# The first input chunk of a decoder trunk in two token halves, its conditioning sums first, and two loads on ScalarE's DMA queue

## Chip, cores and metric

The kernel runs on one core of one Trainium2 chip. The metric is the device time of one launch in microseconds (us): the median of several runs. The program is written directly for the engines: TensorE (PE), VectorE (DVE), ScalarE (ACT), GpSimd (POOL) and SyncE (SP), each with its own stream of instructions, tied to the others by semaphores alone.

## What is computed

A causal decoder trunk of two layers on one sequence: `x` is 512 tokens by 1024, `c` one conditioning vector of 1024, everything in f32. Each layer has a mixer and a SwiGLU feed-forward part, and each of these takes an input that is scaled and shifted by numbers computed from `c`:

```python
c_act = jax.nn.silu(c)
mod = c_act @ ada_w[layer] + ada_b[layer]
sh_m, sc_m, g_m, sh_f, sc_f, g_f = [t[:, None, :] for t in jnp.split(mod, 6, axis=-1)]
hm = x * (1.0 + sc_m) + sh_m
y = gla_mlstm_mixer(hm, ...)        # layer 0; it begins with proj = h @ w_in
x = layer_norm(RES_ALPHA * x + (1.0 + g_m) * y, ...)
```

The mixer of layer 0 (gated linear attention beside an mLSTM) and of layer 1 (stick-breaking beside dilated attention), the feed-forward parts and the norms behind them are not touched. What matters here is the very start: before the first projection can run, `silu(c)` has to be multiplied with the shift and scale blocks of `ada_w[0]` (1024 x 1024 each), and `x` has to be scaled.

## The kernel before

**Layout and arithmetic.** The hidden input h is kept transposed: 1024 features are eight chunks (KC = 8) of 128 partitions, each with 512 tokens. Every f32 product is made of three faster ones: h and the weights are split in a high part in the type fp32r and a low part that is the rest. So for each chunk ACT makes `tmp` (scaled x, L815) and `h_hi` (a copy in fp32r, L800), and DVE makes `h_lo` = tmp - h_hi (`lo_of_chunk`, L1934). Weights come as 512 KB slots of 128 x 1024 in order of use, through a ring of four raw buffers; ACT makes `w_hi` (`hi_until`, L786) and, for the first six slots, DVE makes `w_lo` (`first_lo`, L2030), for the later ones POOL (L728). PE then does three matmuls for each product.

**The start.** SP issues all loads of the start on its queue, in this order: `vec` (110 KB: c, biases), eight pieces of 256 KB of `ada_first` for the first two chunks of the output (`load_pair(0, k, 2)`, L573: for each pair of input chunks k, k+1 one piece of the shift block and one of the scale block), weight slot 0 (L590), x for chunks 0 and 1 (`load_x(0)`, L579), slot 1, then eight such pieces for chunks 2 and 3, x for them, slot 2, and so on. `p` counts these pairs of chunks, 0 to 3.

**The conditioning sums of a pair p** go partly to PE and partly to DVE. PE multiplies the 128 x 128 blocks of `ada_first` with one column of c_act (`first_row`, L1399): for p = 0 the input chunks 0 to 3, for later pairs only chunk 7 (`FIRST_ON_PE`). DVE sums the other input chunks into `ada_acc`, one instruction of 512 columns each (`first_block`, L2009 and L2012: four for p = 0, seven for the others, each waiting for the one before). At the end four closing matmuls with a column of ones (L1413, each two records in the profile) turn DVE's sums into columns and add them to PE's in PSUM: shift and scale (`blk`) for both chunks (`c`) of the pair. DVE then writes shift and scale, `mod` and `scl`, for two chunks at a time (`first_mod`, L2019 and L2020).

**The order of the work** is written out by hand in each engine's stream.

- ACT: c_act (L807), w_hi of slot 0, then for each pair tmp and h_hi of both chunks; w_hi of slot 1 stands between chunk 0 and chunk 1, further slots behind each pair.
- DVE: the four sums of pair 0, w_lo of slot 0, `first_mod(0)`, h_lo of chunk 0, w_lo of slot 1, three sums of pair 1, h_lo of chunk 1, the other four sums of pair 1, w_lo of slot 2, `first_mod(1)`, and on in that manner.
- PE: `first_cols(0)` (the sums of pair 0), then for each chunk k a wait for `h_ready`, then `first_va` (L1424 to L1426: for each of the four token blocks of 128 three matmuls of 512 columns, tokens as the stationary side) and `first_qa` (six matmuls). Ahead of the work of chunk 1 stands `first_cols(1)`, ahead of that of chunk 3 `first_cols(2)`, ahead of that of chunk 5 `first_cols(3)`:

```python
pe.wait_ge(sem("h_ready"), H_BASE["in"] + k + 1)
if k % 2 and p < 3:
    first_cols(p + 1)
for part in (first_qa, first_va) if k % 4 == 3 else (first_va, first_qa):
```

After this start the program goes on through the narrow projection, the other projections and the rest of the two layers.

Of the kernel before, what the change touches and what calls it, by code (L numbers as in the profile page):

```python
# [17 lines left out]
ALU = mybir.AluOpType  # L18
# [176 lines left out]
def build_program(nc, wstream, astream, xT, vecs, const, const0, wa_up, dsel, rel, ln_rows, out):  # L195
# [3 lines left out]
    def sem(name):  # L199
        if name not in sems:  # L200
            sems[name] = ctx.enter_context(nc.semaphore(name))
        return sems[name]
# [362 lines left out]
    def _(sp):  # L565
# [56 lines left out]
        for k in range(0, KC, 2):  # L622
            load_pair(0, k, 2)
        load(0)
        load_x(0)
        load(1)
# [142 lines left out]
    def _(act):  # L769
# [32 lines left out]
        def warm_sqrt():  # L802

            nc.scalar.activation(warm[:], eps_col, ACT.Sqrt)

        act.wait_ge(sem("in_vec"), 16)
        nc.scalar.activation(c_act[:], vec[:, V_C:V_C + KC], ACT.Silu).then_inc(sem("c_ready"), 1)  # L807
        def x_scaled(n):

            if n % 2 == 0:  # L810
                act.wait_ge(sem("first_mod"), n // 2 + 1)
                act.wait_ge(sem(f"in_x{n // 2}"), 16)
            if n >= 2:
                act.wait_ge(sem("h_ready"), n - 1)
            nc.scalar.activation(tmp[:, n % 2, :], x_in[:, n, :], ACT.Identity, scale=scl[:, 0, n:n + 1], bias=mod[:, 0, n:n + 1]  # L815
                                 ).then_inc(sem("h_tmp_ready"), 1)

        hi_until(1)
        for p in range(4):
            for n in (2 * p, 2 * p + 1):  # L820
                x_scaled(n)
                hi_of_chunk(H_BASE["in"] + n, n)
                if n == 0:
                    hi_until(2)
            hi_until((3, 5, 6, 8)[p])
# [364 lines left out]
    def _(pe):  # L1190
# [202 lines left out]
        def first_row(p, k, o, start, stop):  # L1393
# [3 lines left out]
            for blk in range(2):  # L1397
                for c in range(2):
                    pe.matmul(o(blk, c), ada_first[:, p, k, blk, tile_of(c)], c_act[:, k:k + 1], start=start and blk == 0 and c == 0,  # L1399
                              stop=stop, skip_group_check=True)  # L1400

        def first_cols(p):

            o = lambda blk, c: ps[:, 6 + p % 2, 2 * blk + c:2 * blk + c + 1]
            if p == 0:
# [3 lines left out]
            pe.wait_ge(sem("first_step"), first_steps(p + 1))  # L1409
            for blk in range(2):  # L1410
                for c in range(2):
                    a = 512 * (p % 2) + 256 * blk + P * c
                    m = pe.matmul(o(blk, c), ada_acc[:, a:a + P], ones[:], start=not FIRST_ON_PE[p] and blk == 0 and c == 0,  # L1413
                                  stop=True, skip_group_check=True)
            m.then_inc(sem("first_cols"), 1)

        def first_va(k):
# [3 lines left out]
            for tb in range(TB):  # L1421
                o = ps[:, tb, :]
                tokens = tile_of(tb)
                pe.matmul(o, h_lo[:, k, tokens], w_hi[:, s % RING, w], start=k == 0, stop=False)  # L1424
                pe.matmul(o, h_hi[:, k, tokens], w_hi[:, s % RING, w], start=False, stop=False)
# [17 lines left out]
        for p in range(4):  # L1443
            for k in (2 * p, 2 * p + 1):
                pe.wait_ge(sem("h_ready"), H_BASE["in"] + k + 1)
                if k % 2 and p < 3:
# [472 lines left out]
    def _(dve):  # L1919
# [95 lines left out]
        def first_mod(p):  # L2015

            n = slice(2 * p, 2 * p + 2)
            dve.wait_ge(sem("first_cols"), p + 1)
# [15 lines left out]
        link(V.tensor_scalar(scale_b1, vec[:, V_ADAB + KC:V_ADAB + 2 * KC], 1.0, None, ALU.add))  # L2034
        dve.wait_ge(sem("c_ready"), 1)
        first_block(0, range(KC))
        first_lo(0)
        for p in range(4):
            first_mod(p)
            if 1 <= p < 3:  # L2040
                first_block(p + 1, range(0, 2))
            lo_of_chunk(H_BASE["in"] + 2 * p, 2 * p)
            if p == 0:
# [684 lines left out]
```

## Time and profile before

| what | value |
|---|---|
| median of 3 runs | 1309.88 us (1309.43 to 1311.03) |
| the profiled execution's own time | 1308.2 us |
| its span, first to last instruction | 1306.4 us |
| busy: PE, DVE, ACT, POOL | 97%, 51%, 36%, 39% |
| mean granted TensorE clock | 0.996 of full speed |
| bytes moved by DMA | 174.72 MB, mean 134 GB/s |

All stretches are counted in us from the start of the span. PE is TensorE's matmuls, PEld its weight loads. L1413 is line 1413 of the kernel. "Idle before" is the time that an engine stood before an instruction, with the instruction that ended it behind the arrow; in the chain of waits each step is followed back from the last one to what released it. PEclk is the clock that the throttle granted to TensorE (1.00 is full). The DMA share is the mean busy share of the core's 16 DMA engines; by the way it is taken it may be read slightly above 1. MB and GB/s are in millions and thousands of millions of bytes; sizes of transfers are in KB of 1024.

### The profile page before, as it was taken

Reading aid. Unit: us, or ns where it says so; the run is one execution under the profiler, and the core shown is the slowest. Engines: PE = TensorE matmul, PEld = TensorE weight load, DVE = VectorE, ACT = ScalarE, POOL = GpSimd, SP = SyncE. Lnnn points to the kernel's source line nnn. Section 1 sums busy time; section 2 is a strip of 40 time slices with the busy share of each in tenths; the row PEclk is TensorE's granted clock in tenths of the full one; section 3 lists DMA queues with packets and bytes.
Section 4 is the critical chain, followed back from the end, with each engine's and each line's share of the span. In section 5 each row is a group of like instructions: output and inputs, shape, how many; then the busy total and the mean of one; then the engine's idle time right before and its main releaser. Section 6 shows DMA issues by size and latency. Waiting matters only on the chain.

```text
span 1306.4 us, 16760 instructions
## 1 busy us (share of the span) xinstructions
PE 1272.3 (97%) x6338; PEld 1058.7 (81%) x6338; DVE 672.8 (51%) x902; ACT 476.0 (36%) x683; POOL 503.0 (39%) x206
## 2 busy tenths in 40 slices
PE   7999999999999999999999999999999999999996
PEld 6878888779788888888887777988888888888885
DVE  5489777888654455410587566677870101010005
ACT  3443354543322222211342566353542222221113
POOL 0243422223645353544154332321354444444445
PEclk9999999999999999999999999999999999999999
DMA  9972653531564646753164521220232223234312
GB/s 346 184 146 80 223 179 83 191 148 52 207 233 158 225 155 221 242 116 97 49 214 158 164 91 65 81 98 33 65 113 96 96 96 96 96 96 145 96 50 64
DMA packets 94122, 174.72 MB, mean 134 GB/s; under 512 B 15803, under 2 KB 62155, under 8 KB 93940
## 3 DMA queue, kind: packets, MB, share of 16 engines
q1 hardware_dynamic: 89872, 170.03, 41.5%
q10 hardware_dynamic: 4196, 3.95, 1.1%
q8 instruction: 37, 0.61, 0.2%
q14 instruction: 17, 0.14, 0.0%
HBM read 171.79 MB, written 4.52 MB: 135 GB/s over the span
## 4 chain that ended last, share of the span: by engine, by line
PE 85%; issue 5%; DVE 5%; POOL 2%; ACT 1%; DMA 1%; DVEq 0%; SPq 0%; POOLq 0%; ACTq 0%
PE ps L1197 15%; PE ps L1198 15%; PE ps L1199 15%; PE ps L1227 6%; PE ps L1229 6%; PE ps L1228 6%; POOL w_lo L728 2%; PE ps L1367 1%; PE ps L1335 1%; PE ps L1337 1%; PE ps L1369 1%; PE ps L1336 1%; PE ps L1368 1%; PE ps L1810 1%; PE ps L1754 1%
## 5 line engine op out<-in xcount | busy, mean ns | idle before, releaser
L728 POOL TENSOR_TENSOR w_lo<-raw,w_hi 128x1024 fp32r<-128x1024 f32 x191 | 476.5, 2504 | 763.5 <-ACT w_hi L786 763.4
L1197 PE MATMUL ps<-h_lo,w_hi 128*128 128x512 f32 (+2 forms) x1064 | 397.8, 374 | 7.1 <-DVE tmp L2310 2.9
L1199 PE MATMUL ps<-h_hi,w_lo 128*128 128x512 f32 (+2 forms) x1064 | 394.4, 371 | 0.0
L1198 PE MATMUL ps<-h_hi,w_hi 128*128 128x512 f32 (+2 forms) x1064 | 394.3, 371 | 0.0
L786 ACT ACTIVATE w_hi<-raw 128x1024 fp32r<-128x1024 f32 x198 | 208.1, 1056 | 470.2 <-PE ps L1229 159.8
L1197 PEld LDWEIGHTS ps<-h_lo,w_hi 128*128 128x128 f32 (+1 forms) x1064 | 200.9, 189 | 45.7 <-issue 5.2
L1199 PEld LDWEIGHTS ps<-h_hi,w_lo 128*128 128x128 f32 (+1 forms) x1064 | 200.8, 189 | 34.7
L1198 PEld LDWEIGHTS ps<-h_hi,w_hi 128*128 128x128 f32 (+1 forms) x1064 | 201.0, 189 | 33.3
L2432 DVE TENSOR_TENSOR tmp<-tmp,ps 128x512 f32<-128x512 f32 x44 | 30.1, 687 | 242.7 <-PE ps L1199 240.5
L1227 PE MATMUL ps<-w_hi,hid_lo 128*128 128x512 f32 x336 | 132.8, 395 | 0.0
L1229 PE MATMUL ps<-w_lo,hid_hi 128*128 128x512 f32 x336 | 132.6, 395 | 0.0
L1228 PE MATMUL ps<-w_hi,hid_hi 128*128 128x512 f32 x336 | 132.6, 395 | 0.0
L1229 PEld LDWEIGHTS ps<-w_lo,hid_hi 128*128 128x128 f32 x336 | 63.2, 188 | 15.0
L1228 PEld LDWEIGHTS ps<-w_hi,hid_hi 128*128 128x128 f32 x336 | 63.2, 188 | 15.0
L1227 PEld LDWEIGHTS ps<-w_hi,hid_lo 128*128 128x128 f32 x336 | 63.2, 188 | 14.9
L2452 DVE SCALAR_TENSOR_TENSOR ada_acc<-ada_raw,c_act,ada_acc 128x1024 f32<-128x1024 f32 x35 | 55.1, 1575 | 30.0 <-DMA ada_raw<-astream 29.5
L1950 DVE SCALAR_TENSOR_TENSOR ada_acc<-ada_raw,c_act,ada_acc 128x1024 f32<-128x1024 f32 x35 | 55.5, 1585 | 27.1 <-DMA ada_raw<-astream 24.7
L2348 DVE TENSOR_TENSOR ps<-ps,gate_ffn 128x1024 f32<-128x1024 f32 x7 | 8.6, 1231 | 112.4 <-PE ps L1229 112.4
L1065 ACT ACTIVATE hid_hi<-tmp 128x512 f32 (+1 forms) x44 | 27.6, 632 | 82.9 <-DVE tmp L2432 82.9
L2436 DVE TENSOR_TENSOR hid_lo<-tmp,hid_hi 128x512 f32 (+1 forms) x44 | 38.3, 877 | 7.8 <-ACT hid_hi L1065 7.6
L1059 ACT ACTIVATE tmp<-ps 128x512 f32<-128x512 f32 x44 | 24.8, 592 | 38.6 <-PE ps L1199 38.6
L2026 DVE TENSOR_TENSOR w_extra<-raw,w_extra 128x1024 fp32r<-128x1024 f32 x1 | 1.2, 1228 | 67.0 <-POOL w_lo L728 67.0
(300 smaller groups left out, 1648.1 us busy)
## 6 DMA issues: line engine op xcount, KB each, us to landing
raw<-wstream SPq DMA_DIRECT2D x205, 512.0 KB, 4.3
ada_raw<-astream SPq DMA_DIRECT2D x80, 512.0 KB, 4.8
ada_first<-astream SPq DMA_DIRECT2D x16, 256.0 KB, 6.4
ada_first<-astream SPq DMA_DIRECT2D x8, 512.0 KB, 9.5
ln_rows<-row_scratch SPq DMA_DIRECT2D x3, 1024.0 KB, 6.6
skew_scratch<-f_scratch ACTq DMA_DIRECT2D x1, 2304.0 KB
xa<-xT SPq DMA_DIRECT2D x4, 512.0 KB, 8.0
out<-xa SPq DMA_DIRECT2D x3, 512.0 KB, 3.5
```

Of the source, the lines that this page charges most:

```text
L728: nc.gpsimd.tensor_tensor(w_lo[:, slot, :], raw[:, slot % RAW, :], w_hi[:, slot, :].bitcast(F32), ALU.subtract).then_inc(sem("w_lo_ready"), 1)
L786: nc.scalar.activation(w_hi[:, slot, :], raw[:, slot, :], ACT.Copy).then_inc(sem("w_hi_ready"), 1)
L1197: pe.matmul(o, w_h, x_l, start=start, stop=False)
L1198: pe.matmul(o, w_h, x_h, start=False, stop=False)
L1199: return pe.matmul(o, w_l, x_h, start=False, stop=stop)
L1227: pe.matmul(o, x_lo, w_h, start=k == 0, stop=False)
L1228: pe.matmul(o, x_hi, w_h, start=False, stop=False)
L1229: m = pe.matmul(o, x_hi, w_l, start=False, stop=k == nk - 1)
L1950: V.scalar_tensor_tensor(ada_acc[:], src, c_act[:, k:k + 1], ada_acc[:], ALU.mult, ALU.add).then_inc(sem("ada_step"), 1)
L2432: V.tensor_tensor(tmp[:, b, :], tmp[:, b, :], ps[:, up + b, :], ALU.mult).then_inc(sem("prod_ready"), 1)
L2436: V.tensor_tensor(at_(hid_lo), tmp[:, b, :], at_(hid_hi).bitcast(F32), ALU.subtract).then_inc(sem("hid_ready"), 1)
L2452: V.scalar_tensor_tensor(ada_acc[:], ada_raw[:, k % 2, :], c_act[:, k:k + 1], ada_acc[:], ALU.mult, ALU.add).then_inc(sem("ada_step"), 1)
```

## The change

Five edits, all at the start:

- SP no longer issues weight slot 0 and x of the first pair. ACT issues both on its own DMA queue as its first instructions, ahead of c_act.
- `first_chunk` takes the place of tmp and h_hi for chunk 0: tmp and h_hi on tokens 0 to 255, then on tokens 256 to 511, each with semaphores of its own (`first_tmp`, `first_hi`). w_hi of slot 1 follows. DVE makes h_lo of chunk 0 in the same two halves, and PE begins when the first half is there (`first_lo`) and waits for `h_ready` ahead of token block 2.
- For pair 0, the closing matmuls of chunk 0 stand in PSUM bank 6 and those of chunk 1 in bank 7; chunk 0's two come first and signal `first_cols_a`. In the other pairs only the order of the four closing matmuls is changed.
- `first_mod(0)` writes shift and scale of chunk 0 after `first_cols_a` and those of chunk 1 after `first_cols`, in two pairs of instructions on one column each. ACT waits for the first before chunk 0 and for the second before chunk 1.
- On DVE, w_lo of slot 0 moves from behind the four sums of pair 0 to ahead of them.

```diff
--- before.py
+++ after.py
@@ -621,8 +621,6 @@
 
         for k in range(0, KC, 2):
             load_pair(0, k, 2)
-        load(0)
-        load_x(0)
         load(1)
         for p in range(1, 4):
             if p == 1:
@@ -803,11 +801,15 @@
 
             nc.scalar.activation(warm[:], eps_col, ACT.Sqrt)
 
+        act.dma_start(raw[:, 0, :], slot_source(0)).then_inc(sem("raw_landed0"), 16)
+        act.dma_start(x_in[:, 0:2, :], xT[0:2 * P].rearrange("(k p) t -> p k t", p=P)).then_inc(sem("in_x0"), 16)
         act.wait_ge(sem("in_vec"), 16)
         nc.scalar.activation(c_act[:], vec[:, V_C:V_C + KC], ACT.Silu).then_inc(sem("c_ready"), 1)
         def x_scaled(n):
 
-            if n % 2 == 0:
+            if n == 1:
+                act.wait_ge(sem("first_mod"), 1)
+            elif n % 2 == 0:
                 act.wait_ge(sem("first_mod"), n // 2 + 1)
                 act.wait_ge(sem(f"in_x{n // 2}"), 16)
             if n >= 2:
@@ -815,13 +817,27 @@
             nc.scalar.activation(tmp[:, n % 2, :], x_in[:, n, :], ACT.Identity, scale=scl[:, 0, n:n + 1], bias=mod[:, 0, n:n + 1]
                                  ).then_inc(sem("h_tmp_ready"), 1)
 
+        def first_chunk():
+
+            act.wait_ge(sem("first_mod_a"), 1)
+            act.wait_ge(sem("in_x0"), 16)
+            for hf in range(2):
+                t = half_of(hf)
+                done = (sem("first_tmp"), sem("h_tmp_ready"))[hf]
+                nc.scalar.activation(tmp[:, 0, t], x_in[:, 0, t], ACT.Identity, scale=scl[:, 0, 0:1], bias=mod[:, 0, 0:1]
+                                     ).then_inc(done, 1)
+                act.wait_ge(done, 1)
+                nc.scalar.activation(h_hi[:, 0, t], tmp[:, 0, t], ACT.Copy).then_inc((sem("first_hi"), sem("h_hi_ready"))[hf], 1)
+
         hi_until(1)
         for p in range(4):
             for n in (2 * p, 2 * p + 1):
+                if n == 0:
+                    first_chunk()
+                    hi_until(2)
+                    continue
                 x_scaled(n)
                 hi_of_chunk(H_BASE["in"] + n, n)
-                if n == 0:
-                    hi_until(2)
             hi_until((3, 5, 6, 8)[p])
 
         def x_chunk(n):
@@ -1396,22 +1412,26 @@
                 pe.wait_ge(sem(f"in_ada{p}_{k // 2 * 2 if p < 2 else k // 4 * 4}"), 32)
             for blk in range(2):
                 for c in range(2):
-                    pe.matmul(o(blk, c), ada_first[:, p, k, blk, tile_of(c)], c_act[:, k:k + 1], start=start and blk == 0 and c == 0,
+                    pe.matmul(o(blk, c), ada_first[:, p, k, blk, tile_of(c)], c_act[:, k:k + 1],
+                              start=start and blk == 0 and (c == 0 or p == 0),
                               stop=stop, skip_group_check=True)
 
         def first_cols(p):
 
-            o = lambda blk, c: ps[:, 6 + p % 2, 2 * blk + c:2 * blk + c + 1]
+            o = ((lambda blk, c: ps[:, 6 + p % 2, 2 * blk + c:2 * blk + c + 1]) if p else
+                 (lambda blk, c: ps[:, 6 + c, 2 * blk + c:2 * blk + c + 1]))
             if p == 0:
                 pe.wait_ge(sem("c_ready"), 1)
             for k in FIRST_ON_PE[p]:
                 first_row(p, k, o, k == FIRST_ON_PE[p][0], False)
             pe.wait_ge(sem("first_step"), first_steps(p + 1))
-            for blk in range(2):
-                for c in range(2):
+            for c in range(2):
+                for blk in range(2):
                     a = 512 * (p % 2) + 256 * blk + P * c
                     m = pe.matmul(o(blk, c), ada_acc[:, a:a + P], ones[:], start=not FIRST_ON_PE[p] and blk == 0 and c == 0,
                                   stop=True, skip_group_check=True)
+                if p == 0 and c == 0:
+                    m.then_inc(sem("first_cols_a"), 1)
             m.then_inc(sem("first_cols"), 1)
 
         def first_va(k):
@@ -1421,6 +1441,8 @@
             for tb in range(TB):
                 o = ps[:, tb, :]
                 tokens = tile_of(tb)
+                if k == 0 and tb == 2:
+                    pe.wait_ge(sem("h_ready"), H_BASE["in"] + 1)
                 pe.matmul(o, h_lo[:, k, tokens], w_hi[:, s % RING, w], start=k == 0, stop=False)
                 pe.matmul(o, h_hi[:, k, tokens], w_hi[:, s % RING, w], start=False, stop=False)
                 m = pe.matmul(o, h_hi[:, k, tokens], w_lo[:, s % RING, w], start=False, stop=k == KC - 1)
@@ -1442,7 +1464,7 @@
         first_cols(0)
         for p in range(4):
             for k in (2 * p, 2 * p + 1):
-                pe.wait_ge(sem("h_ready"), H_BASE["in"] + k + 1)
+                pe.wait_ge(*((sem("h_ready"), H_BASE["in"] + k + 1) if k else (sem("first_lo"), 1)))
                 if k % 2 and p < 3:
                     first_cols(p + 1)
                 for part in (first_qa, first_va) if k % 4 == 3 else (first_va, first_qa):
@@ -2014,6 +2036,13 @@
 
         def first_mod(p):
 
+            if p == 0:
+                for c in range(2):
+                    dve.wait_ge(sem("first_cols" if c else "first_cols_a"), 1)
+                    V.tensor_tensor(mod[:, 0, c:c + 1], ps[:, 6 + c, c:c + 1], vec[:, V_ADAB + c:V_ADAB + c + 1], ALU.add)
+                    V.tensor_tensor(scl[:, 0, c:c + 1], ps[:, 6 + c, 2 + c:3 + c], scale_b1[:, c:c + 1], ALU.add
+                                    ).then_inc(sem("first_mod" if c else "first_mod_a"), 1)
+                return
             n = slice(2 * p, 2 * p + 2)
             dve.wait_ge(sem("first_cols"), p + 1)
             V.tensor_tensor(mod[:, 0, n], ps[:, 6 + p % 2, 0:2], vec[:, V_ADAB + 2 * p:V_ADAB + 2 * p + 2], ALU.add)
@@ -2033,13 +2062,20 @@
         dve.wait_ge(sem("in_vec"), 16)
         link(V.tensor_scalar(scale_b1, vec[:, V_ADAB + KC:V_ADAB + 2 * KC], 1.0, None, ALU.add))
         dve.wait_ge(sem("c_ready"), 1)
+        first_lo(0)
         first_block(0, range(KC))
-        first_lo(0)
         for p in range(4):
             first_mod(p)
             if 1 <= p < 3:
                 first_block(p + 1, range(0, 2))
-            lo_of_chunk(H_BASE["in"] + 2 * p, 2 * p)
+            if p == 0:
+                for hf in range(2):
+                    t = half_of(hf)
+                    dve.wait_ge(sem("h_hi_ready" if hf else "first_hi"), 1)
+                    V.tensor_tensor(h_lo[:, 0, t], tmp[:, 0, t], h_hi[:, 0, t].bitcast(F32), ALU.subtract
+                                    ).then_inc(sem("h_ready" if hf else "first_lo"), 1)
+            else:
+                lo_of_chunk(H_BASE["in"] + 2 * p, 2 * p)
             if p == 0:
                 first_lo(1)
                 first_block(1, range(0, 2))
```

## Rows read from the trace of the kernel before

**Rows 1.** The page: span, and TensorE's busy time, share and instructions
```profile
span 1306.4 us, 16760 instructions
...
PE 1272.3 (97%) x6338; PEld 1058.7 (81%) x6338; DVE 672.8 (51%) x902; ACT 476.0 (36%) x683; POOL 503.0 (39%) x206
```

**Rows 2.** Chain of waits, 0 to 25 us: start, duration, what
```profile
1.67 3.93 DMA ada_first<-astream
...
5.74 6.96 PE ps L1399 x32
12.69 1.72 PE ps L1413 x8
...
17.15 1.23 DVE w_lo L2030
...
23.43 0.76 DVE ada_acc L2012
```

**Rows 3.** Timeline of PE: start, duration, line, operation, [idle before <-releaser]
```profile
16.95 0.80 PE L1424 MATMUL ps<-w_hi,h_lo 128*128 128x512 f32 x1 [2.55 <-DVE h_lo L1934]
17.55 0.63 PE L1425 MATMUL ps<-w_hi,h_hi 128*128 128x512 f32 x1
...
20.11 0.43 PE L1425 MATMUL ps<-w_hi,h_hi 128*128 128x512 f32 x1
...
24.23 1.05 PE L1413 MATMUL ps<-ones,ada_acc 128*128 128x1 f32 x8 [0.64 <-DVE ada_acc L2012]
...
63.62 0.47 PE L1197 MATMUL ps<-h_lo,w_hi 128*128 128x512 f32 x1 [0.41 <-POOL w_lo L728]
```

**Rows 4.** Timeline of DVE, ACT and SP's queue, 0 to 17 us
```profile
0.74 1.28 ACT L807 ACT_TABLE_LOAD   x1 [0.74 <-PEq L2722]
...
2.81 0.21 ACT L807 ACTIVATE c_act<-vec 128x8 f32<-128x8 f32 x1 [0.79 <-DMA vec<-vecs]
...
5.25 0.50 SPq L590 DMA_DIRECT2D raw<-wstream  x1
...
5.80 0.50 SPq L579 DMA_DIRECT2D xa<-xT  x1
...
9.35 0.49 DVE L2009 TENSOR_SCALAR ada_acc<-ada_first,c_act 128x512 f32<-128x512 f32 x1 [6.12 <-DMA ada_first<-astream]
9.87 2.40 DVE L2012 SCALAR_TENSOR_TENSOR ada_acc<-ada_first,c_act,ada_acc 128x512 f32<-128x512 f32 x3
...
13.03 1.23 DVE L2030 TENSOR_TENSOR w_lo<-raw,w_hi 128x1024 fp32r<-128x1024 f32 x1 [0.76 <-ACT w_hi L786]
...
14.70 0.81 ACT L815 ACTIVATE tmp<-xa,mod,scl 128x512 f32<-128x512 f32 x1 [1.70 <-DVE scl L2020]
...
15.54 0.63 ACT L800 ACTIVATE h_hi<-tmp 128x512 fp32r<-128x512 f32 x1
16.08 1.04 ACT L786 ACTIVATE w_hi<-raw 128x1024 fp32r<-128x1024 f32 x1
```

**Rows 5.** Lines L985 and L2317: half-width h_hi and h_lo, ns min/median/max
```profile
L985 ACT ACTIVATE h_hi<-tmp x48: 397/418/422, 279.8 to 945.1; 128x256 fp32r<-128x256 f32 x48
...
L2317 DVE TENSOR_TENSOR h_lo<-tmp,h_hi x48: 409/416/2319, 280.5 to 945.6; 128x256 fp32r<-128x256 f32 x48
```

**Rows 6.** Busy by stretch: us, engines' busy time, PEclk, DMA share, GB/s
```profile
2.00:6.00 4.00, 0.26 (x2) 0.29 (x2) 0.17 (x1) 0.23 (x2) 0.00 (x0) 1.00 0.92 267
6.00:12.00 6.00, 6.00 (x30) 6.00 (x29) 2.48 (x4) 0.06 (x1) 0.00 (x0) 1.00 0.96 339
12.00:17.00 5.00, 2.45 (x13) 2.36 (x12) 2.41 (x5) 3.27 (x4) 0.00 (x0) 1.00 1.07 393
24.00:46.00 22.00, 21.77 (x116) 18.73 (x117) 17.84 (x29) 9.18 (x12) 0.00 (x0) 1.00 1.05 398
```

**Rows 7.** Line L506, one of ACT's own DMA issues, ns min/median/max
```profile
L506 ACTq DMA_DIRECT2D bt<-skew_scratch x3: 399/521/529, 745.1 to 746.1; - x3
```

**Rows 8.** Two later holes of PE, and the stretch behind the longer
```profile
243.48 1.28 PE L1584 MATMUL ps<-cst,og 128*128 128x128 f32 x8 [2.37 <-DVE h_lo L2242]
...
281.47 0.38 PE L1197 MATMUL ps<-h_lo,w_hi 128*128 128x256 f32 x1 [2.86 <-DVE tmp L2310]
...
283.30:286.80 3.50, 3.42 (x17) 3.42 (x18) 3.46 (x9) 2.49 (x5) 0.00 (x0) 0.55 0.00 0
```

## The prediction

> **What bounds the kernel now.** The page comes first: TensorE (PE) is busy for 97% of the 1306.4 us span [rows 1]. So time at the start is worth something only if PE's stream moves with it; whatever the change does lies before the first matmuls and in the 8 us behind them. The profiled execution took 1308.2 us, 1.8 more than its span, and the three runs have a median of 1309.88 (1309.43 to 1311.03): the profiled one is the fastest seen. I work out a difference on its trace and put it on the median. About 0.2%, or 2.62 us, is what a measurement of this kernel can tell from no change.
>
> The chain of waits of the first 25 us [rows 2] reads: the first ada_first pieces land at 5.60, the conditioning sums on PE run from 5.74 to 14.41 without a hole (6.96 and 1.72 us), then DVE mod and scl, ACT tmp, ACT h_hi, ACT w_hi of the second weight slot (to 17.12), DVE w_lo, and DVE's seven steps for the next two chunks until 24.19; PE's next closing sums start at 24.23. PE's timeline [rows 3] adds that it does its first matmuls from 16.95 beside this and then stands 0.64 us for DVE. They come 0.427 apart (17.55 to 20.11, six), which is the lower of PE's two levels, 1.2 GHz, behind a hole of 2.55; that slow stretch lies in DVE's shade. **So the first matmul at 16.95 isn't what sets the time; DVE's chain from 17.15 to 24.19 is.** From 24.23 on PE has no hole until one of 0.41 us at 63.62 [rows 3], and the POOL work named there waits for weight copies that ACT makes behind PE's own output. A shift at 24.23 therefore goes through to the end, one for one.
>
> **The change, part by part.** The terms are for the start of that DVE chain.
>
> *Two token halves.* Before, from the start of ACT tmp (14.70) to that of w_hi (16.08) are 0.84 for tmp and 0.54 for h_hi [rows 4]. A 512-column copy takes 0.63 and a 256-column one 0.42 (L985) [rows 4, 5], so a half is worth 0.21 less. In its place stand tmp, h_hi, tmp, h_hi on halves: 2 x (0.63 + 0.33) = 1.92 instead of 1.38. The next w_hi starts **0.54 later** after the modulation, and DVE's w_lo and all behind it with it. The first matmul gains: 0.29 for mod and scl, 0.63, about 0.45, 0.41 for a half h_lo (L2317) [rows 5] and 0.06 make 1.84 where 2.54 passed (14.41 to 16.95), so 0.7. PE then has 1.5 us more in hand at a place where it waits for DVE anyway: worth nothing. DVE's extra h_lo half (0.41) lies while ACT makes the second w_hi: nothing. Token blocks 2 and 3 wait for the second half; it is there about 1.0 us after the first, and the six matmuls ahead of it take 2.56 (0.427 each, 16.95 to 19.51) [rows 3]: nothing, and 0.4 if half the matmuls' time were gone.
>
> *Conditioning sums of chunk 0 first.* Two of four closing matmuls (four of eight records at 0.215 [rows 2]) are enough for the scale: **0.86 earlier**. The second pair of DVE adds (under 0.29) lies beside ACT's first half. The other bank and the start flags cost nothing.
>
> *w_lo of slot 0 ahead of the sums on DVE.* It stood at 13.03 to 14.26, under PE's sums [rows 4]. With the scale 0.86 earlier it would have stuck out by 0.7; moved, it needs slot 0 landed by about 7 to be done (1.06 + 1.23) before DVE's first sum at 9.35. Behind it on DVE stand all the sums. Taken at nothing; if slot 0 is late by x beyond the slack of 0.4 that DVE has at 12.27 against 12.69, it costs x less that.
>
> *Two loads on ACT's queue.* SP loses 0.50 + 0.50 us of issue behind the eight ada_first issues [rows 4], so slot 1 and all later issues go out 1.05 earlier; DMA is full until 46 us (share 1.05 at 398 GB/s) [rows 6], so that brings no bytes forward. ACT gains two issues ahead of its table load and of the activation c_act that every sum needs; its DMA issues take 0.40 to 0.53 [rows 7], so c_act, which ran from 2.81 to 3.02 [rows 4], comes up to 1.06 later, at 4.1; vec may land later still beside raw slot 0. Both are ahead of the pieces' landing at 5.60: nothing, unless vec takes 1.5 us more. **What costs is bytes:** raw slot 0 and x, 0.524 MB each, now go out at 0.74, before the ada_first pieces and beside them. From 2 to 6 us the engines have a share of 0.92 at 267 GB/s, from 6 to 12 0.96 at 339 [rows 6]: there is hardly room beside ada_first. I work out the delay of PE's sums twice.
>
> First pieces: vec and the first two (0.113 + 0.524 MB) have passed, at these rates, at 4.3 and land at 5.60, lag 1.3. If the queues share evenly, 1.274 MB must pass. At 339 GB/s that is at 5.7, landing 7.0: +1.4. At the old rates +2.2; at 398 +0.8; if the moved loads go wholly ahead +1.8 (398) to +3.4 (old rates).
> Last pieces: before, 2.21 MB; after, 3.26 MB, whichever queue wins. DVE needs 1.53 us behind them, and its sums must be done for PE at 12.69. With 339 GB/s for the first 6 us and then 393 (12 to 17 us [rows 6], where more ada_first pieces move with a backlog): passed at 11.05, landing 12.65 (lag 1.6, as for the third pair), DVE done 14.2: +1.5. At 398 throughout +0.6, at the old rates +2.8.
> I take **+1.5**, for which both agree, since the mixed traffic of 6 to 12 us is the nearest row. The bounds are 0 (nothing disturbed) and 3.4.
>
> Here the Trainium skill speaks against the change. DMA: Bandwidth & Descriptors, "Issuing engines are not separate DMA queues", says that transfers started by different engines run on the same 16 DMA engines and interleave, so that a second issuer saves only issue time. The shares above 0.9 agree; by that page alone the delay is the full even share at the old rates, +2.2, and the sum would be +1.9. No run yet shows the two queues side by side at the start.
>
> **Sum:** +1.5 - 0.86 + 0.54 = **+1.2 us**: 1309.4 against the profiled 1308.2, 1311.1 on the median.
>
> **Rivals.** (a) *The second queue fills the engines.* Deeper backlog lifts 267 GB/s to what the 24 to 46 us row shows and order does the rest; delay 0. For it: full rates are seen with the same ada_first pieces later. Against: share 0.92 already. Result 0.54 - 0.86 = -0.3: 1309.6.
> (b) *The moved megabyte is paid in full* (the one that ends slower). Place: ACT's queue from 0.74 against the first ada_first pair. If the 4 KB rows of raw and 2 KB rows of x go ahead of the 1 KB rows, and the rate stays as it was, the pair lands 3.4 later, the last pieces 2.8: +2.5 to +3.1, 1312.4 to 1313.0. It decides against me from a delay of 2.94. The same page's "Queues, rings and completion order" has an engine finish a whole packet of one queue before it switches, which would favour the larger rows; no row here shows two queues at once.
> (c) *A longer hole costs PE its clock.* By my terms PE reaches the second closing sums 0.86 + 0.7 = 1.56 earlier against its first sums, DVE only 0.32, so PE waits there for 0.64 + 1.56 - 0.32 = 1.9 us. After a hole of 2.86 us at 278.6 the granted clock fell to 0.55 from 283.3 to 286.8, near the lower level of 1.2 GHz; that cost 0.45 x 3.5 = 1.6 us [rows 8]. A hole of 2.37 at 243.48 [rows 8] and the present one of 0.64 weren't followed by such a stretch. So it may go either way; with my sum it makes +2.8, 1312.7, decided by whether the clock column falls within some microseconds behind 25.
> (d) *It doesn't do what it says:* the second half's wait holds PE, or slot 0 is late on DVE. The slack of 1.5 speaks against; result within 0.5 of mine.
> (e) *Faster by over 0.2%.* The most that rows allow is -0.3, and -1.6 if the clock drop at 283 us also falls away; only with the spread of the runs (1.6) does that reach -2.62.
>
> **How the numbers follow.** My case (delay 0.6 to 2.2, +0.3 to +1.9) 0.50; (a) 0.16; (b) 0.13; (c) 0.15; (d) 0.03; (e) 0.03. Slower by over 0.2%: two thirds of (b), over half of (c): 0.17. Faster: (e) and a trace of (a), 0.04. The same: 0.79. The range goes from (a) less half the runs' spread, 1308.7, to the end of (b) and (c) with the same, 1313.7.
>
> **What would show it.** In the changed kernel's timeline: first L1399 later than 5.74 (6.5 to 8); ACT's first tmp about 0.6 later than 14.70; the half tmp and h_hi at 0.60 and 0.42; w_hi of slot 1 starting 1.9 after the first half tmp; L1413 of the second pair at about 25.4, after a wait of 1.9 for ada_acc; from there all rows shifted alike. The forecast is wrong if the sums start at 5.74 (then a), if w_lo of slot 1 doesn't follow ACT directly, or if the shift at 24.23 isn't found at the end.

## The result and the profile after

| | before | changed |
|---|---|---|
| median | 1309.56 us (14 runs, 1307.74 to 1311.03) | 1313.81 us (14 runs, 1310.30 to 1315.74) |
| profiled execution, its span | 1308.20, 1306.4 | 1311.02, 1309.2 |
| its granted clock | 0.996 | 0.996 |
| ratio | | 1.0029, interval 1.0022 to 1.0036 |

The change makes the kernel slower by 0.29%, some 3.8 us (the two medians lie 4.25 apart, the two means 3.96), and the whole interval lies above the 0.2% that the forecast had set as its bound. Its likeliest case, no change that can be measured, was wrong, and so was its sum, +1.2; its range held the result only by its upper edge. The page of the changed kernel answers to [rows 1]:

```profile
span 1309.2 us, 16765 instructions
...
PE 1273.3 (97%) x6338; PEld 1059.5 (81%) x6338; DVE 674.0 (51%) x905; ACT 476.6 (36%) x685; POOL 502.1 (38%) x206
```

The chain of waits of its first 27 us answers to [rows 2]; columns are start, duration, what:

```profile
1.67 6.70 DMA ada_first<-astream
...
8.51 6.95 PE ps L1415 x32
15.46 0.87 PE ps L1431 x4
...
16.61 0.61 ACT tmp L827
...
17.24 0.42 ACT h_hi L830
17.66 0.50 ACT tmp L827
...
18.18 0.42 ACT h_hi L830
18.59 0.96 ACT w_hi L784
...
19.57 1.23 DVE w_lo L2059
...
25.85 0.76 DVE ada_acc L2034
```

Read it against the chain before. The first pieces of ada_first land at 8.37 instead of 5.60: **+2.77 us**. PE's sums take the same 6.95. Then four records of the closing sums, 0.87, are enough instead of 1.72 for eight. Then tmp, h_hi, tmp, h_hi on halves and the copy of slot 1; DVE's w_lo of slot 1 starts at 19.57 instead of 17.15, +2.42. DVE's seven steps end at 26.61 instead of 24.19, +2.42.

The timeline shows the engines around it, first ACT with its own DMA queue, then DVE, then PE (start, duration, and in brackets the idle time before, with what ended it), and answers to [rows 3, 4]:

```profile
0.75 0.43 ACTq L804 DMA_DIRECT2D raw<-wstream  x1
1.20 0.47 ACTq L805 DMA_DIRECT2D xa<-xT  x1
...
4.99 0.21 ACT L807 ACTIVATE c_act<-vec 128x8 f32<-128x8 f32 x1 [2.00 <-DMA vec<-vecs]
...
6.50 1.23 DVE L2059 TENSOR_TENSOR w_lo<-raw,w_hi 128x1024 fp32r<-128x1024 f32 x1 [1.10 <-ACT w_hi L784]
11.13 0.49 DVE L2031 TENSOR_SCALAR ada_acc<-ada_first,c_act 128x512 f32<-128x512 f32 x1 [3.40 <-DMA ada_first<-astream]
11.65 2.39 DVE L2034 SCALAR_TENSOR_TENSOR ada_acc<-ada_first,c_act,ada_acc 128x512 f32<-128x512 f32 x3
...
18.17 0.79 PE L1446 MATMUL ps<-w_hi,h_lo 128*128 128x512 f32 x1 [1.00 <-DVE h_lo L2075]
...
22.60 0.63 PE L1447 MATMUL ps<-w_hi,h_hi 128*128 128x512 f32 x1
...
23.66 0.40 PE L1214 MATMUL ps<-h_hi,w_hi 128*128 128x512 f32 x1
...
26.66 1.05 PE L1431 MATMUL ps<-ones,ada_acc 128*128 128x1 f32 x8 [0.89 <-DVE ada_acc L2034]
...
66.01 0.47 PE L1213 MATMUL ps<-h_lo,w_hi 128*128 128x512 f32 x1 [0.41 <-POOL w_lo L726]
```

ACT's two loads go out at 0.75 and 1.20. c_act, which waits for `vec`, runs at 4.99 instead of 2.81: even `vec`, issued at the same moment on SP's queue, was pushed back by over 2 us. w_lo of slot 0 (6.50) costs nothing in its new place, DVE's sums end at 14.04, ahead of PE's rows at 15.46. PE's first matmul is at 18.17 instead of 16.95, its matmuls are still the slow ones (0.63) at 22.60 and the fast ones (0.40) at 23.66, PE waits 0.89 for DVE's last step, and from there the shift runs through: the hole that was at 63.62 [rows 3] is at 66.01, +2.39. PE's holes at 220.85, 243.48, 281.47 and 331.32 before lie at 223.23, 245.87, 284.00 and 334.22 after, +2.4, +2.4, +2.5, +2.9. The last half microsecond lies in the holes from 281 to 334 us: those at 281.47 and 331.32 are 0.13 and 0.21 longer, and one of 0.17 is new at 285.90. The spans differ by 2.8.

The stretches answer to [rows 6]; behind the engines' busy time stand the granted clock, DMA share and GB/s:

```profile
2.00:6.00 4.00, 0.00 (x0) 0.00 (x0) 0.17 (x1) 1.89 (x3) 0.00 (x0) 1.00 0.83 284
6.00:12.00 6.00, 3.50 (x17) 3.53 (x17) 2.06 (x3) 0.37 (x1) 0.00 (x0) 1.00 1.08 386
```

With two queues at work the first four microseconds move 284 GB/s instead of 267; the 386 against 339 of the next six come too late for the first pieces. It isn't the second queue that brings the few GB/s: e3 below has the same loads on one queue and moves 311 GB/s from 2 to 6 us.

How the two queues shared the engines stands in the counts of each queue: packets, MB, and their share of the engines' time. Of the changed kernel's trace, first from 3 to 4 us and then from 5 to 7 us (q10 is ACT's queue, q1 is SP's):

```profile
q10 hardware_dynamic: 72, 0.29, 71.6%
q1 hardware_dynamic: 74, 0.06, 21.8%
...
q10 hardware_dynamic: 218, 0.43, 59.9%
q1 hardware_dynamic: 261, 0.25, 38.2%
```

ACT's queue did not go strictly first: both moved all the time, and **nearly packet for packet**. A row of the transfer is about one packet here (ACT's queue counts 416 packets for its 384 rows), so the queue with the larger rows gets more bytes: nearly five times as many while raw slot 0 (rows of 4 KB) passes beside `vec` (rows of 880 bytes), 1.7 times as many while x (2 KB) passes beside ada_first (1 KB). e1 (78 to 77 from 3 to 4 us, 217 to 225 from 5 to 7) and e9 (67 to 63, 227 to 265) show the same. `vec` and the first two pieces are 688 packets with what each transfer adds to its rows, ACT's two loads 416: by the time that the pieces are through, at about 7.4 us, all of ACT's megabyte has passed too.

### The profile page after: what moved, and what is told of

Same layout as the page of the kernel before. It is cut to its first block, busy times and chain, and to the rows that moved or that the text cites. A ratio compares the mean times of both kernels' runs of the same rounds, so it can differ in the third digit from the quotient of the medians.

```text
span 1309.2 us, 16765 instructions
## 1 busy us (share of the span) xinstructions
PE 1273.3 (97%) x6338; PEld 1059.5 (81%) x6338; DVE 674.0 (51%) x905; ACT 476.6 (36%) x685; POOL 502.1 (38%) x206
## 4 chain that ended last, share of the span: by engine, by line
PE 84%; issue 5%; DVE 5%; POOL 2%; ACT 1%; DMA 1%; DVEq 0%; SPq 0%; POOLq 0%; ACTq 0%
PE ps L1213 15%; PE ps L1215 15%; PE ps L1214 15%; PE ps L1245 6%; PE ps L1243 6%; PE ps L1244 6%; POOL w_lo L726 2%; PE ps L1383 1%; PE ps L1351 1%; PE ps L1353 1%; PE ps L1385 1%; PE ps L1384 1%; PE ps L1352 1%; PE ps L1832 1%; PE ps L1776 1%
```

## The experiments

All were timed against the kernel before on the same chip. "First sum" is the start of PE's first conditioning sum, "w_lo 1" that of DVE's w_lo of slot 1, "second sums" that of the second closing sums on PE, all in the profiled execution.

| run | median | ratio, interval | first sum | w_lo 1 | second sums |
|---|---|---|---|---|---|
| before, in its groups of runs | 1309.56 to 1309.84 | | 5.74 | 17.15 | 24.23 |
| changed | 1313.81 | 1.0029, 1.0022 to 1.0036 | 8.51 | 19.57 | 26.66 |
| e1, loads on ACT's queue only | 1312.66 | 1.0023, 1.0013 to 1.0032 | 8.47 | 19.89 | 26.98 |
| e3, same loads first on SP's queue | 1312.93 | 1.0028, 1.0016 to 1.0039 | 8.64 | 20.06 | 27.23 |
| e8, slot 0 only on ACT's queue | 1311.55 | 1.0015, 1.0006 to 1.0025 | 6.73 | 18.14 | 25.23 |
| e4, changed, loads after the first pair | 1311.67 | 1.0013, 1.0003 to 1.0022 | 5.39 | 20.17 | 27.26 |
| e2, changed, loads back on SP | 1310.38 | 1.0003, 0.9993 to 1.0013 | 5.22 | 16.30 | 23.38 |
| e7, halves only | 1310.90 | 1.0007, 0.9998 to 1.0016 | 5.59 | 17.52 | 24.60 |
| e5, chunk 0's sums first only | 1308.70 | 0.9994, 0.9985 to 1.0003 | 5.64 | 16.20 | 23.36 |
| e6, e5 and a row of sums to DVE | 1308.45 | 0.9988, 0.9979 to 0.9997 | 5.67 | 16.11 | 23.19 |
| e9, changed once more | 1313.23 | 1.0027, 1.0018 to 1.0036 | 8.50 | 19.58 | 26.66 |

### The two loads alone, on ACT's queue (e1)

```diff
--- before
-        load(0)
-        load_x(0)
...
+        act.dma_start(raw[:, 0, :], slot_source(0)).then_inc(sem("raw_landed0"), 16)
+        act.dma_start(x_in[:, 0:2, :], ...).then_inc(sem("in_x0"), 16)
         act.wait_ge(sem("in_vec"), 16)
```

> The kernel before with the two loads on ACT's queue and nothing else. Theory (the moved megabyte is paid in full): the first conditioning sum starts at 8.5 us instead of 5.74, as in the changed kernel, DVE's w_lo of slot 1 at about 19.9 (+2.75), profiled span +2.7 us against before; it is slower than the changed kernel by the 0.3 that halves and early sums gained for DVE's chain. Rival (the halves and the waits on one column cost the time): the first sum at 8.5 but the time within 1 us of before. For the clock: if the late start alone brings the extra throttled stretches, the runs of this kernel scatter by 4 to 5 us as those of the changed one.

The timeline of this kernel, PE and DVE:

```profile
8.47 6.96 PE L1399 MATMUL ps<-c_act,ada_first 128*128 128x1 f32 x32 [8.47 <-DMA ada_first<-astream]
...
19.89 1.23 DVE L2030 TENSOR_TENSOR w_lo<-raw,w_hi 128x1024 fp32r<-128x1024 f32 x1 [0.25 <-ACT w_hi L784]
```

First sum 8.47, w_lo of slot 1 19.89, +2.74 with +2.75 expected, with no halves and no early sums in the kernel. The time is 0.23% above before. So the loads carry the loss, and the distance from the first sum to w_lo of slot 1 (11.42) is that of before (11.41). The ten runs scatter from 1310.39 to 1315.90, by 5.5 us, as the changed kernel's do (5.4); that the late start alone goes with such a scatter had been named ahead, and the section on the clock comes back to it.

### The same bytes first, on one queue (e3)

```diff
--- before
+        load(0)
+        load_x(0)
         for k in range(0, KC, 2):
             load_pair(0, k, 2)
-        load(0)
-        load_x(0)
         load(1)
```

> The kernel before with slot 0 and x issued ahead of the eight ada_first pieces on SP's own queue; one queue. Theory (bytes ahead cost, the second queue only lets them go ahead): first sum at 8.5 to 9.5 and the span +2.7 to +3.8 us. Rival (it is the second queue, not the bytes): first sum later than 5.74 by under 1.5 us.

```profile
8.64 6.96 PE L1399 MATMUL ps<-c_act,ada_first 128*128 128x1 f32 x32 [8.64 <-DMA ada_first<-astream]
...
20.06 1.23 DVE L2030 TENSOR_TENSOR w_lo<-raw,w_hi 128x1024 fp32r<-128x1024 f32 x1 [0.26 <-ACT w_hi L786]
```

First sum 8.64. With everything on SP's queue, slot 0 and x strictly ahead, the pieces are 0.17 later than with two queues. **It isn't the second queue but the megabyte that passes before the pieces are through.** Two queues that start together treat ada_first about as badly here as a strict order would, though by another way: in turns, packet for packet, as the counts above show. An even share of the bytes is no description of what happened. `vec` is early here (c_act at 2.81) and the first sum no earlier, so the late `vec` of the changed kernel cost nothing.

### Half the bytes (e8)

```diff
--- before
-        load(0)
         load_x(0)
...
+        act.dma_start(raw[:, 0, :], slot_source(0)).then_inc(sem("raw_landed0"), 16)
         act.wait_ge(sem("in_vec"), 16)
```

> The kernel before with only weight slot 0 on ACT's queue, x stays on SP's behind the ada_first pieces: half of the moved bytes. If the moved bytes are paid in full, the delay halves: first sum at 7.1 us (+1.4), span +1.4 us. If the larger 4 KB rows are what pushes ada_first back, nearly the whole 2.7 us comes from slot 0 alone: first sum at 8 or later.

```profile
6.73 6.96 PE L1399 MATMUL ps<-c_act,ada_first 128*128 128x1 f32 x32 [6.73 <-DMA ada_first<-astream]
...
18.14 1.22 DVE L2030 TENSOR_TENSOR w_lo<-raw,w_hi 128x1024 fp32r<-128x1024 f32 x1 [0.26 <-ACT w_hi L785]
```

First sum 6.73: +1.0 against the profiled execution of before, +1.0 to +1.5 against the 5.22 to 5.74 of the six profiles whose first pieces had nothing beside them. That is near the half (+1.4 was expected) and far from the whole; the 4 KB rows of slot 0 alone aren't what costs 2.7. Time +0.15%. The spread of half a microsecond in the landing doesn't let me say whether it is somewhat less than proportional. The queues' counts are again nearly packet for packet (84 on ACT's queue to 81 on SP's from 3 to 4 us), and all of slot 0 has passed by 5 us.

### The loads held back until the first pair has landed (e4)

```diff
--- changed
-        act.dma_start(raw[:, 0, :], ...)
-        act.dma_start(x_in[:, 0:2, :], ...)
         act.wait_ge(sem("in_vec"), 16)
         nc.scalar.activation(c_act[:], ...)
+        act.wait_ge(sem("in_ada0_0"), 32)
+        act.dma_start(raw[:, 0, :], ...)
+        act.dma_start(x_in[:, 0:2, :], ...)
...
+                    if c == 0:
+                        first_lo(0)
...
-        first_lo(0)
         first_block(0, range(KC))
```

Here and in e2, w_lo of slot 0 stands on DVE between the modulation of chunk 0 and that of chunk 1.

> The changed kernel, but ACT issues its two loads only when the first pair of ada_first has landed, about where SP issued them before; w_lo of slot 0 between the two modulation columns. Theory: two queues cost nothing once the first pieces are through: first sum at 5.74, w_lo of slot 1 at 16.8 to 17.3, span within 0.5 us of before. Rival (a second queue always takes its share from the later pieces): DVE's four sums end over 1 us later than 12.27 and the closing sums start over 1 us late.

The timeline of ACT's queue, PE, DVE and PE again:

```profile
5.28 0.41 ACTq L807 DMA_DIRECT2D raw<-wstream  x1
...
5.39 6.96 PE L1416 MATMUL ps<-c_act,ada_first 128*128 128x1 f32 x32 [5.39 <-DMA ada_first<-astream]
...
14.30 1.54 DVE L2035 SCALAR_TENSOR_TENSOR ada_acc<-ada_first,c_act,ada_acc 128x512 f32<-128x512 f32 x2 [1.15 <-DMA ada_first<-astream]
...
15.89 1.44 PE L1432 MATMUL ps<-ones,ada_acc 128*128 128x1 f32 x6 [3.54 <-DVE ada_acc L2035]
```

My theory missed here. The first sum is back at 5.39, but DVE, which sums input chunks 4 to 7, now stands 1.15 us for its pieces and ends at 15.84, and PE's closing sums wait 3.54 us for it. Its first piece comes late already: the first of its sums stands until 11.88, which was at 9.35. The loads were issued at the same time as before, 5.28; yet before they stood *behind* all eight pieces on one queue, here beside what was left of them. What the rival of this run foretold, sums and closing sums over 1 us late, is there. Its reason, that the second queue takes its share from the later pieces, isn't shown: by 10 us ACT's queue had moved only 0.12 MB, and SP's 2.15 MB against 2.32 before. So few bytes don't explain a third pair that lands 2.5 us late; why the last packets of these pieces came so late stays open. w_lo of slot 1 is as late as in e1. The time is up by 0.13% (interval to 0.22%), less than the +3.0 of the trace; this profiled execution, 1313.16 us, was the slowest of the ten runs, so its landing times are probably at the late end.

### The changed kernel with its loads back (e2)

```diff
--- changed
+        load(0)
+        load_x(0)
         load(1)
...
-        act.dma_start(raw[:, 0, :], ...)
-        act.dma_start(x_in[:, 0:2, :], ...)
...
+                    if c == 0:
+                        first_lo(0)
...
-        first_lo(0)
         first_block(0, range(KC))
```

> The changed kernel with both loads back on SP's queue in their old place, and w_lo of slot 0 on DVE between the two modulation columns. Theory: first sum back at 5.74, w_lo of slot 1 at 16.8 to 16.9 (-0.3), PE's first matmul at 15.4 to 15.9, span 0.3 us below before; PE's hole before the second closing sums grows to about 1.9 us. Rival (the halves cost the time): it stays 2 us or more above before. Clock rival: the longer hole at 22 to 24 us brings a granted clock well under 1 in the 4 us behind it, in some runs, and the time then lies 1.5 to 3 us above before.

```profile
5.22 6.96 PE L1415 MATMUL ps<-c_act,ada_first 128*128 128x1 f32 x32 [5.22 <-DMA ada_first<-astream]
...
16.30 1.23 DVE L2061 TENSOR_TENSOR w_lo<-raw,w_hi 128x1024 fp32r<-128x1024 f32 x1 [0.52 <-ACT w_hi L786]
...
23.38 1.05 PE L1431 MATMUL ps<-ones,ada_acc 128*128 128x1 f32 x8 [1.35 <-DVE ada_acc L2034]
```

Against the first sum, w_lo of slot 1 is at 11.08 instead of 11.41: -0.33, with -0.32 worked out. The rest of the profiled execution's gain comes from pieces that happened to land 0.5 earlier. PE's first matmul is at 14.95, 1.48 earlier against the first sum than before, and PE then stands 1.35 before the second closing sums instead of 0.64; 1.9 was expected. Behind this hole the granted clock is 1.00 from 23 to 31 us, so the clock rival isn't seen in this execution. The time is that of before (1.0003). With this the loss of the changed kernel is its loads' alone, as far as these runs can tell.

### Halves only, and early sums only (e7, e5)

e7, against e2:

```diff
-                    dve.wait_ge(sem("first_cols" if c else "first_cols_a"), 1)
+                    dve.wait_ge(sem("first_cols"), 1)
...
-                    if c == 0:
-                        first_lo(0)
...
         first_block(0, range(KC))
+        first_lo(0)
```

> Only the token halves: chunk 0's modulation waits for all closing sums as before, w_lo of slot 0 behind DVE's sums as before. Term of the prediction: w_lo of slot 1 is 0.54 us later against the first sum (11.95 behind it instead of 11.41), PE's first matmul 0.7 earlier, the hole before the second closing sums 1.9 us, span +0.5 us at one clock. Rival (the halves bring the work forward): the second closing sums start 0.5 or more earlier than before.

```profile
5.59 6.96 PE L1415 MATMUL ps<-c_act,ada_first 128*128 128x1 f32 x32 [5.59 <-DMA ada_first<-astream]
...
17.52 1.23 DVE L2059 TENSOR_TENSOR w_lo<-raw,w_hi 128x1024 fp32r<-128x1024 f32 x1 [0.52 <-ACT w_hi L786]
...
24.60 1.05 PE L1431 MATMUL ps<-ones,ada_acc 128*128 128x1 f32 x8 [0.85 <-DVE ada_acc L2034]
```

e5, against e2:

```diff
-            for hf in range(2):
-                nc.scalar.activation(tmp[:, 0, t], x_in[:, 0, t], ACT.Identity, ...)
-                nc.scalar.activation(h_hi[:, 0, t], tmp[:, 0, t], ACT.Copy)
+            nc.scalar.activation(tmp[:, 0, :], x_in[:, 0, :], ACT.Identity, ...)
+            hi_of_chunk(H_BASE["in"], 0)
```

with one h_lo on DVE and one wait on PE for chunk 0 again.

> Only the sums of chunk 0 first, no token halves, loads in their old place on SP's queue. By the terms of the prediction this keeps the 0.86 us and drops the 0.54 of the halves: w_lo of slot 1 about 0.86 earlier against the first sum than before (10.55 us behind it instead of 11.41), second closing sums 0.86 earlier, span -0.9 us against before when both are at one clock; PE's hole ahead of the second closing sums stays near 0.6. Rival (PE's first matmul sets the time): the gain is not larger than that of the kernel with halves.

```profile
5.64 6.96 PE L1411 MATMUL ps<-c_act,ada_first 128*128 128x1 f32 x32 [5.64 <-DMA ada_first<-astream]
...
16.20 1.23 DVE L2055 TENSOR_TENSOR w_lo<-raw,w_hi 128x1024 fp32r<-128x1024 f32 x1 [0.25 <-ACT w_hi L786]
...
23.36 1.03 PE L1427 MATMUL ps<-ones,ada_acc 128*128 128x1 f32 x8
```

The distances from the first sum to w_lo of slot 1 are 11.93 and 10.56, expected were 11.95 and 10.55. So the halves alone cost 0.52 and the early sums alone give 0.85. The halves bring PE's first matmul forward and lengthen the path that counts: PE stands 0.85 before the second closing sums in e7. In e5 DVE's chain gained so much that PE doesn't wait for it any more (a hole near 0.6 was expected): its second closing sums are 0.77 earlier against the first sum than before, not 0.85, since PE's own stream now sets them. The times go the same way, 1.0007 and 0.9994, but both intervals include 1, so they alone don't show either term.

### A version that beats both (e6)

e5, and one more row of the first sums goes from PE to DVE, which has nothing to do until 9.35 [rows 4]:

```diff
--- e5
-    FIRST_ON_PE = ((0, 1, 2, 3), (7,), (7,), (7,))
+    FIRST_ON_PE = ((0, 1, 2), (7,), (7,), (7,))
...
-                if p < 2 and k % 2 == 0 or k % 4 == 0:
-                    dve.wait_ge(sem(f"in_ada{p}_{k}"), 32)
+                if p < 2 and (k % 2 == 0 or k == first) or k % 4 == 0:
+                    dve.wait_ge(sem(f"in_ada{p}_{k // 2 * 2 if p < 2 else k}"), 32)
```

> As the one before, and DVE takes the fourth row of the first conditioning sums from PE (PE rows 0 to 2, DVE rows 3 to 7). DVE has time before 9.35 us for it; PE's rows end after 5.2 us instead of 6.96, and the closing sums then wait for DVE's last step at 12.27 to 12.3: 0.4 more gained, span -1.3 us against before at one clock, median 1308.3. Rival (the last ada_first pieces or w_lo of slot 0 bind instead): the closing sums of this kernel start no earlier than in the one before, and it gains nothing further.

The timeline of DVE, PE and DVE:

```profile
8.96 1.54 DVE L2028 SCALAR_TENSOR_TENSOR ada_acc<-ada_first,c_act,ada_acc 128x512 f32<-128x512 f32 x2 [0.72 <-DMA ada_first<-astream]
10.75 1.54 DVE L2028 SCALAR_TENSOR_TENSOR ada_acc<-ada_first,c_act,ada_acc 128x512 f32<-128x512 f32 x2 [0.26 <-DMA ada_first<-astream]
...
12.35 1.87 PE L1427 MATMUL ps<-ones,ada_acc 128*128 128x1 f32 x8 [1.43 <-DVE ada_acc L2028]
...
16.11 1.22 DVE L2055 TENSOR_TENSOR w_lo<-raw,w_hi 128x1024 fp32r<-128x1024 f32 x1 [0.25 <-ACT w_hi L786]
```

The median is 1308.45, ratio 0.9988 (0.9979 to 0.9997): below both kernels and, by its interval, faster than the one before, by 0.12%, which is still within the 0.2% named ahead. Against e5 the runs alone show no difference. The row that DVE took over gave less than worked out: DVE stands 0.72 and 0.26 for pieces, its last step ends at 12.29, and w_lo of slot 1 is 10.44 behind the first sum, 0.12 better than e5 and not 0.4. The last pieces bind, as the rival said; most of the gain is that of the early sums.

### The clock (e9)

The changed kernel again, without an edit.

> The changed kernel once more, unchanged, for its clock. So far its 14 runs have a mean granted clock of 0.9941 against 0.9947 in 61 runs of the kernel before, and its median lies 1.3 us above what the 2.4 to 2.8 us of its trace explain. If the change brings more throttled stretches, the mean clock is again 0.9941 or less and the median near 1313.8. If that was chance, the mean clock is 0.9947 and the median near 1312.5, 2.8 above before; its fastest runs, at 0.996, lie 2.5 to 3 above the fastest of before in either case.

Every run lists its mean granted clock. Over 25 runs of the changed kernel (14 and 11) the mean is 0.9941, over the 77 runs of the kernel before that stood beside the experiments 0.9947; 11 of 25 are at 0.993 or below against 13 of 77. Within one kernel the clock goes with the time:

| clock | before, mean (runs) | changed, mean (runs) | difference |
|---|---|---|---|
| 0.996 | 1308.7 (23) | 1311.4 (6) | 2.7 |
| 0.994, 0.995 | 1309.8 (41) | 1312.9 (8) | 3.1 |
| 0.993 and below | 1311.1 (13) | 1314.6 (11) | 3.5 |

So at one clock the changed kernel is 2.7 to 3.5 us slower, about the 2.8 of the two profiled spans, and about half a microsecond of the mean comes from its lower clock. The three other kernels whose first sum is late (e1, e3, e8) lie at 0.9942 over 27 runs, the five others (e2, e4 to e7) at 0.9948 over 52; the lower clock seems to go with the late loads, a grouping made after the fact. The profile of e9 caught a throttled stretch at a place where neither [rows 3] nor the changed kernel's first profile has one. Stretches of it, the clock being the third column from the right:

```profile
25.00:27.00 2.00, 1.33 (x12) 1.20 (x12) 1.90 (x3) 0.00 (x0) 0.00 (x0) 1.00 1.09 397
27.00:30.50 3.50, 3.50 (x13) 2.98 (x13) 2.81 (x7) 2.15 (x3) 0.00 (x0) 0.54 1.04 413
...
33.00:40.00 7.00, 7.00 (x41) 6.09 (x40) 4.78 (x8) 0.73 (x2) 0.00 (x0) 1.00 1.07 406
```

and PE's timeline there:

```profile
26.66 1.33 PE L1431 MATMUL ps<-ones,ada_acc 128*128 128x1 f32 x8 [0.67 <-DVE ada_acc L2034]
...
29.28 0.63 PE L1446 MATMUL ps<-w_hi,h_lo 128*128 128x512 f32 x1
29.71 0.63 PE L1447 MATMUL ps<-w_hi,h_hi 128*128 128x512 f32 x1
```

PE has the closing sums behind a hole of 0.67, little else from 25 to 27, and then a granted clock of 0.54 for 3.5 us: matmuls come 0.43 apart, the lower level of 1.2 GHz, where they are 0.23 apart at full clock. This costs 0.46 x 3.5 = 1.6 us, at the place that rival (c) had named. That a longer hole brings it isn't shown: this one is 0.67, and behind those of 1.35 (e2) and 1.34 (e4) the clock stayed at 1.00. Other throttled stretches lie at 240 to 250, 280 to 290 and 680 to 700 us, in some profiles and not in others: e5 has them at 240 and 680, the kernel before at 280. The kernel needn't differ for it: of the changed kernel's two profiles, the first has one of them, at 285, and e9 those at 245 and 685. Whether the changed kernel draws them more often, or 25 runs fell that way, these runs make likely and don't settle.

## Where the prediction was right and where it was wrong, point by point

- **That DVE's chain sets the time and a shift there goes through one for one:** right. +2.42 at w_lo of slot 1, +2.39 at 66.01, +2.8 in the span. e7 shows it best: against the first sum, PE's first matmul is 0.69 earlier and the second closing sums are 0.52 later.
- **Halves, +0.54 on that chain:** measured +0.52 (e7). **Early sums, -0.86:** measured -0.85 (e5). Together -0.33 (e2) and -0.35 (changed, 19.57 - 8.51 = 11.06 against 11.41). w_lo of slot 0 ahead of the sums: nothing, as taken.
- **The loads on ACT's queue, taken at +1.5:** this is the step that failed; it measured +2.77. It was mis-sized, by its first half, the first pieces. I let the queues share their bytes evenly and took 339 GB/s of the later row; in the place where it counted the chip moved 284 GB/s, and the queues took turns by packets, so that all of slot 0 and x passed before the pieces were through. Put back into the same working: 1.686 MB at 284 GB/s until 6 us and 386 behind it have passed at 7.4 and land, with the lag of 1.3, at 8.7; found 8.37. By an even share it would have been 1.274 MB at 6.3, landing at 7.6. The upper end that I had written down, 3.4, had the right bytes and the old rates; that both ways of working it out agreed on +1.5 was chance. The last pieces were sized well: DVE done at 14.2 worked out, 14.04 found; they didn't bind, since PE's rows ended later.
- **Rival (b), the megabyte is paid in full,** is what happened, at the place given and at less than the price: the first pair landed 2.77 later for the 3.4 given, DVE's sums, which follow the last pieces, ended 1.77 later (14.04 for 12.27) for 2.8. It had a chance of 0.13. The delay alone, under the 2.94 from which it was to decide, puts the traces at +2.4 to +2.8, about at the bound of 0.2%; the rest of the 3.8 goes with the lower clock. The result lies at the very end of the range: 1313.81 is 0.1 above it, and 0.29% on the median that the forecast started from is 1313.7. That the range reaches so far was half luck: its end is 1313.0 for (b) at the old rates, +3.1, which the traces didn't reach, and half the spread of the runs, 0.8; the lower mean clock that goes with the rest is in neither. The hint for more was in the rows: at a DMA share of 0.92 nothing is free. Rival (a), full engines and no delay, is refuted by e1 (first sum at 8.47).
- **Rival (c), a throttled stretch behind the hole at the second sums,** exists (e9), in some executions, but behind a hole of 0.67; longer ones in e2 and e4 had none. In the changed kernel the hole was 0.89 and not the 1.9 I had worked out, because PE's matmuls stayed 0.43 apart for 5 us (18.17 to 23.03) instead of 3 (to 20.11 [rows 3]); that took most of what it had in hand. By the table the lower clock is worth half a microsecond of the mean, if it is no chance.
- **The Trainium skill,** DMA: Bandwidth & Descriptors, "Issuing engines are not separate DMA queues": e1 and e3 agree (8.47 and 8.64): issuing from ACT brought no bandwidth, only a place beside the first pieces. The page speaks of interleaving and the counts of packets agree; that this means an even share of the bytes was my reading, and it doesn't hold. With "Queues, rings and completion order", by which an engine finishes a packet of one queue before it takes the next, the turns in the counts (72 to 74, 218 to 261) and the late `vec` (c_act at 4.99) fit. How many rows make such a turn these counts, taken over all 16 engines, don't show.

## What to carry to other kernels

A transfer has no price of its own where the DMA engines are full; it has the price of what stands behind it. Before moving a load to another engine's queue, add its bytes ahead of the transfer that the first instruction of the critical chain waits for, at the rate of that stretch, and don't count on a fair share of bytes: count packets (here about one for each row) on both queues, and take all bytes of the other queue that its packets cover. And before speeding up the first matmul, look whether PE waits again further on: splitting a tile in halves helps who consumes it and costs who stands behind it on the producing engine.

## What the runs showed of the hardware

- Two DMA queues started together shared by packets, not by bytes: 72 packets on ACT's queue to 74 on SP's from 3 to 4 us, 218 to 261 from 5 to 7 us, with 0.29 to 0.06 MB and 0.43 to 0.25 MB. With 1.05 MB in rows of 4 and 2 KB on ACT's queue, the first 0.52 MB of ada_first in rows of 1 KB on SP's landed at 8.37, within 0.3 of a strict order behind it (e3: 8.64 for the sum that follows). With half the bytes the first sum started at 6.73.
- Rates at the start are lower than later: 267 GB/s from 2 to 6 us on one queue with rows of 1 KB, 284 on two queues, 311 on one queue with the larger rows first (e3), against 393 from 12 to 17 us [rows 6].
- With two loads issued on a second queue at 5.28 us, in the middle of a backlog, pieces issued earlier on the first queue came so late that PE stood 3.54 us (e4, one execution), although the second queue had moved only 0.12 MB by 10 us. The cause is open.
- The landing of the same first transfers varies by half a microsecond between executions (first sums at 5.22 to 5.74).
- Throttled stretches come in some executions and not in others, of one kernel too (at 285 us in one profile of the changed kernel; at 27, 245 and 685 in the other); the two looked at closely cost about 1.6 us each. Of the variance of the times, 0.53 goes with the mean clock in the kernel before (77 runs) and 0.73 in the changed one (25 runs).
